# Last layer of a decoder trunk: the residual stored to the output early, and the experts' rows added to it by indirect DMAs, one per expert of a unit and one behind the other

## The reference, cut to what matters

```
def hybrid_layer(x, ...):
    ...
    h = x + mix @ w_o
    return h + hierarchical_moe(rmsnorm(h, norm2_g), w_rg, b_rg, w_re, b_re, w1, w3, w2)

def hierarchical_moe(...):
    # top-1 of 4 groups, then top-2 of its 8 experts: 2 experts a token, 32 in all, no capacity limit
    def expert_block(args):
        xb, e = args
        hid = jax.nn.silu(xb @ w1[e]) * (xb @ w3[e])      # 1024 -> 256
        return hid @ w2[e]                                  # 256 -> 1024
    ...
    y = jnp.zeros((T, d), xn.dtype).at[buf_tok].add(ybuf * buf_gate[:, None])
```

## Time and profile before

| | |
|---|---|
| median of 3 runs (lowest, highest) | 2005.02 us (2003.66, 2007.26) |
| profiled execution, first to last instruction (span) | 2003.5 us |
| PE busy | 1841.7 us (92%) |
| DVE, ACT, POOL busy | 712.4, 555.0, 327.6 us |
| DMA, mean over the span | 163 GB/s, 325.73 MB |
| last layer: h part, unit part, adding | about 1534 to 1685, 1685 to 1968, 1968 to 2003.5 us |

### The profile page before, as it was taken

How to read it: one execution, slowest core, us unless ns; L and a number is a source line. 1 busy time by engine, 2 the same in 40 slices (tenths; PEclk the granted TensorE clock), 3 DMA queues, 4 the chain that set the end, 5 groups by cost and what they waited for, 6 DMA issues and landing times. The chain is left out here.

```text
span 2003.5 us, 29201 instructions
## 1 busy us (share of the span) xinstructions
PE 1841.7 (92%) x11200; PEld 1013.5 (51%) x11200; DVE 712.4 (36%) x2085; ACT 555.0 (28%) x1313; POOL 327.6 (16%) x372
## 2 busy tenths in 40 slices
PE   7999998999899889998699999899998997999992
PEld 4555555776645443333255555567675554433330
DVE  0111105667634522222212221266764443222224
ACT  2121216665612211110121111266563222111010
POOL 0332321011100011111013332310210000111110
PEclk9999998999999989999899999999999997999996
DMA  7000000002061289999752110100203315999997
GB/s 262 11 22 11 0 21 32 1 1 96 2 260 64 105 318 415 423 417 416 277 176 84 43 53 0 53 2 1 85 12 129 147 64 215 356 422 422 415 364 305
DMA packets 93208, 325.73 MB, mean 163 GB/s; under 512 B 19856, under 2 KB 33808, under 8 KB 76688
## 3 DMA queue, kind: packets, MB, share of 16 engines
q1 hardware_dynamic: 70416, 272.97, 34.9%
q0 software_dynamic: 12096, 33.57, 4.2%
q10 hardware_dynamic: 10560, 17.33, 2.5%
HBM read 295.52 MB, written 38.80 MB: 167 GB/s over the span
## 5 line engine op out<-in xcount | busy, mean ns | idle before, releaser
L437 PE MATMUL banks<-r_win,r_tile 128*128 128x384 f32 (+3 forms) x1536 | 531.4, 505 | 9.4 <-DMA r_win<-in_w_in 7.2
L437 PEld LDWEIGHTS banks<-r_win,r_tile 128*128 128x128 f32 x1536 | 292.7, 192 | 226.8 <-issue 61.6
L1827 PE MATMUL banks<-r_win,r_proj 128*32 128x512 f32 (+2 forms) x1184 | 255.3, 606 | 7.9 <-DVE r_proj L2148 4.3
L1675 PE MATMUL banks<-r_proj,r_tile 128*128 128x512 f32 x512 | 238.2, 607 | 0.2 <-DVE r_proj L2098 0.2
L1107 ACT ACTIVATE r_win<-r_win 128x256 f32<-128x256 f32 (+7 forms) x256 | 177.3, 695 | 28.3 <-DVE r_win L1179 20.7
L1827 PE MATMUL banks<-r_proj 128*32 128x512 f32 (+1 forms) x736 | 157.1, 596 | 8.7 <-DMA r_win<-in_w 3.8
L990 PE MATMUL banks<-r_win 64*128 64x512 f32 (+3 forms) x704 | 136.1, 506 | 19.6 <-DVE r_win L1151 10.3
L1675 PEld LDWEIGHTS banks<-r_proj,r_tile 128*128 128x128 f32 x512 | 93.1, 193 | 94.2 <-issue 93.7
L1001 PE MATMUL banks<-fixed,r_win 128*128 128x128 f32 x984 | 132.4, 280 | 6.6 <-ACT r_win L1115 6.5
L1001 PEld LDWEIGHTS banks<-fixed,r_win 128*128 128x128 f32 x984 | 106.2, 141 | 49.5 <-issue 42.8
L507 ACT ACTIVATE r_proj<-banks,rx 128x384 f32<-128x384 f32 (+1 forms) x80 | 48.1, 601 | 297.2 <-PE banks L437 297.2
(11 more groups left out here) (229 smaller groups left out, 2114.9 us busy)
## 6 DMA issues: line engine op xcount, KB each, us to landing
r_win<-in_w SPq DMA_DIRECT2D x99, 1024.0 KB, 18.5
r_proj<-in_w SPq DMA_DIRECT2D x60, 1024.0 KB, 21.6
r_tile<-in_w SPq DMA_DIRECT2D x33, 1024.0 KB, 19.0
r_win<-in_w_in SPq DMA_DIRECT2D x6, 1536.0 KB, 18.3
r_proj<-in_w_o SPq DMA_DIRECT2D x2, 4096.0 KB, 13.4
residual<-r_tile ACTq DMA_DIRECT2D x16, 512.0 KB, 2.9
out<-r_tile SPq DMA_DIRECT2D x16, 512.0 KB, 8.2
r_win<-expert_rows SPq DMA_DIRECT2D x16, 512.0 KB, 9.7
```

Of the source, the lines that this page charges most:

```text
L437: mm = pe.matmul(bk[b][:, 0:CHUNKS[c]], uT[j][:, k, :], w_ch[c][:, k, :], start=(k == 0), stop=(k == KT - 1))
L1675: mm = pe.matmul(bk[2 * (t % 2) + c][:, :], mix[t][:, k, :], s.w_o[:, k, 512 * c:512 * c + 512], start=(k == 0), stop=(k == KT - 1))
L1827: mm = pe.matmul(bk[2 + j][at, 0:2 * F].rearrange("p (c n) -> p c n", c=2), xT[j][:, k, at], w13[c][:, :, k, :], start=(k == 0), stop=(k = ...
```

## The change

1. In the last layer ACT stores each tile of `h` a second time, to `out`, right behind the store to `residual` (in `scale`). SP (before its loads of the experts 5 and 6) and POOL (before its first gather) wait until all 8 of these have landed.
2. The scatter of a unit to `expert_rows` becomes `add_rows`: for each expert of the unit (each "piece") one indirect DMA from the same `y_t` buffer to `out`, which adds instead of overwriting (`compute_op=ALU.add`). A new table `piece_rows` has the slots of the other piece past the end, so that they are left out; it costs one more DVE operation and one more wait behind `rows_out`, in both layers, and a constant table of 42 columns in `fixed`. Each of these DMAs is issued only when the one before it has landed: the second piece of a unit waits for the first, the first for the last piece of the unit before. There are 2 units of one piece and 19 of two, so 40 such DMAs.
3. `first_half` and `second_half` wait, before they overwrite a `y_t` buffer, for both pieces of unit n-2.
4. The reload of `h`, the read-back, the adds on DVE and the stores to `out` at the end are gone. The pass ends when all pieces have landed.
5. `cum`, a small table of the attention, moves into the weight buffer to make room, and counters are added for the passes of this layer.

```
@@ scale
                 act.dma_start(rows(s.h_dram, t), h_t[t]).then_inc(g.hs.sem, 16)
+                if last_layer:
+                    act.dma_start(rows(s.out_f, t), h_t[t]).then_inc(g.os.sem, 16)
@@ block.sync
                 sp.wait_ge(g.hs.sem, g.hs.at(layer, 16 * NT))
+                if last_layer:
+                    sp.wait_ge(g.os.sem, 16 * NT)
...
-                        else:
-                            for t in tiles_at_sets(s):
-                                sp.dma_start(h_t[t], rows(s.h_dram, t)).then_inc(g.hb.sem, 16)
...
-            if last_layer:
-                for t in range(NT):
-                    for k in range(2):
-                        sp.dma_start(yg[t][k], rows(s.y_dram, k * NT + t)).then_inc(g.yg[t].sem, 16)
-                for t in range(NT):
-                    sp.wait_ge(g.ad.sem, 2 * (t + 1))
-                    sp.dma_start(rows(s.out_f, t), h_t[t]).then_inc(g.st.sem, 16)
-                sp.wait_ge(g.st.sem, 16 * NT)
@@ block.gpsimd
+            if last_layer:
+                wait_alone(pool, s, g.os.sem, 16 * NT)
+            def add_rows(n):
+                j, col = n % 2, units[n].col
+                for i in range(len(units[n].pieces)):
+                    if i > 0:
+                        wait_alone(pool, s, g.ac[j].sem, g.ac[j].at(here, added(units, n) - 16))
+                    elif n > 0:
+                        wait_alone(pool, s, g.ac[1 - j].sem, g.ac[1 - j].at(here, added(units, n - 1)))
+                    nc.gpsimd.indirect_dma_start(
+                        out=s.out_f, out_offset=bass.IndirectOffsetOnAxis(
+                            ap=piece_rows[:, U * i + col:U * i + col + 1], axis=0),
+                        in_=y_t[j], in_offset=None, bounds_check=NT * P - 1, oob_is_err=False,
+                        compute_op=ALU.add).then_inc(g.ac[j].sem, 16)
...
-                        scatter(n - 4)
+                        if last_layer:
+                            add_rows(n - 4)
+                        else:
+                            scatter(n - 4)
@@ first_half (second_half the same with dve)
                     if n >= 2:
-                        act.wait_ge(g.ys[j].sem, g.ys[j].at(done, 16 * (n // 2)))
+                        wait_rows_out(act, n - 2)
@@ new
+    def wait_rows_out(eng, n):
+
+        j = n % 2
+        if last_layer:
+            eng.wait_ge(g.ac[j].sem, g.ac[j].at(count_here(eng), added(units, n)))
+        else:
+            eng.wait_ge(g.ys[j].sem, g.ys[j].at(count(eng), 16 * (n // 2 + 1)))
+
+def added(units, n):
+
+    return 16 * sum(len(u.pieces) for u in units[n % 2:n + 1:2])
@@ rows_out
                 v.scalar_tensor_tensor(out=slot_rows[:, 0:U], in0=row_less, scalar=SKIP, in1=bk[0][:, 0:U],
-                                       op0=ALU.add, op1=ALU.add).then_inc(g.ix.sem, 1)
+                                       op0=ALU.add, op1=ALU.add).then_inc(g.sr.sem, 1)
+                wait_alone(dve, s, g.sr.sem, n)
+                ins = v.tensor_tensor(piece_rows.rearrange("p (i u) -> p i u", i=2),
+                                      bcast(slot_rows[:, 0:U].unsqueeze(1), [P, 2, U]),
+                                      s.other_piece.rearrange("p (i u) -> p i u", i=2), ALU.add)
+                ins.then_inc(g.ix.sem, 1)
@@ after the last unit, DVE
-            if last_layer:
-                for t in range(NT):
-                    dve.wait_ge(g.yg[t].sem, 32)
-                    for k in range(2):
-                        v.tensor_tensor(h_t[t], h_t[t], yg[t][k], ALU.add).then_inc(g.ad.sem, 1)
```

More of the change, by code:

```diff
@@ L90, in trunk @@
         banks = [bank_pairs[b // 2][:, 512 * (b % 2):512 * (b % 2) + 512] for b in range(8)]
-        fixed = sb("fixed", [P, 5 * P + 2 * NT * (NROPE // 2) + 1 + 2 * NT + 2])
+        units_n = len(plan_units(E)[0])
+        fixed = sb("fixed", [P, 5 * P + 2 * NT * (NROPE // 2) + 1 + 2 * NT + 2 + 2 * units_n])
         ident, ones, upto, before = (fixed[:, n * P:(n + 1) * P] for n in range(4))
         iota = fixed[:, 4 * P:5 * P]
-        after = itertools.accumulate((5 * P, NT * NROPE, 1, 2 * NT, 1, 1))
-        cos_sin, pick, targets, key_col, expert_col = (fixed[:, a:b] for a, b in itertools.pairwise(after))
+        after = itertools.accumulate((5 * P, NT * NROPE, 1, 2 * NT, 1, 1, 2 * units_n))
+        cos_sin, pick, targets, key_col, expert_col, s_other = (fixed[:, a:b] for a, b in itertools.pairwise(after))
         cos_sin = cos_sin.rearrange("p (a t c) -> p a t c", a=2, t=NT)
@@ L117, in trunk @@
         fox = sb("fox", [P, 3, NT, HEADS])
-        cum = sb("cum", [P, NT, HEADS])
+        cum = r_win[:, 19104:19136].rearrange("p (t h) -> p t h", h=HEADS)
         nrounds = sb("nrounds", [1, 1], I32)
@@ L216, in trunk @@
         s.rounds_done = rounds_done
-        s.reloads = nc.sync.alloc_register("reloads")
         s.attend_sems = attend_sems
         s.route_sems = route_sems
+        s.rounds_here = {e.engine: e.alloc_register("rounds_here") for e in (nc.sync, nc.scalar, nc.vector, nc.gpsimd, nc.tensor)}
         s.rounds = {e.engine: e.alloc_register("rounds") for e in (nc.sync, nc.scalar, nc.vector, nc.gpsimd, nc.tensor)}
@@ L1328, in __init__ @@
         self.col, self.ranks, self.slots = col, ranks, slots
+        self.pieces = [(blocks[0][0], blocks[-1][1]) for blocks in slots]
 def plan_units(experts_n):
@@ L1429, in route_signals @@
     g.ys = [sig(f"expert_rows_stored{j}", 16 * even[j]) for j in range(2)]
+    g.ac = [sig(f"expert_rows_added{j}", added(units, U - 2 + (U + j) % 2)) for j in range(2)]
+    g.os = sig("output_seeded", 16 * NT)
     g.nv = sig("next_pass_places_ready", 2 * NT)
@@ L1527, in count, with count_here, wait_all_rows_out @@
         return eng.snap(s.rounds_done[eng.engine])
+    def count_here(eng):
+        return eng.snap(s.rounds_here[eng.engine])
+    def wait_rows_out(eng, n):
[4 more added lines that the diff above has]
+            eng.wait_ge(g.ys[j].sem, g.ys[j].at(count(eng), 16 * (n // 2 + 1)))
+    def wait_all_rows_out(eng):
+        for j in range(2):
+            if last_layer:
+                wait_alone(eng, s, g.ac[j].sem, g.ac[j].at(count_here(eng), g.ac[j].per_pass))
+            else:
+                wait_alone(eng, s, g.ys[j].sem, g.ys[j].at(count(eng), g.ys[j].per_pass))
     def next_round(eng):
         eng.reg_add(s.rounds_done[eng.engine], s.rounds_done[eng.engine], 1)
+        eng.reg_add(s.rounds_here[eng.engine], s.rounds_here[eng.engine], 1)
         eng.wait_ge(g.nr.sem, g.nr.at(layer, 4))
@@ L1652, in _ @@
             with passes(pool):
-                done = count(pool)
+                done, here = count(pool), count_here(pool)
                 wait_alone(pool, s, g.ix.sem, g.ix.at(done, 1) + layer)
@@ L1931, in _ @@
                 if not last_layer:
-                    for j in range(2):
-                        wait_alone(act, s, g.ys[j].sem, g.ys[j].at(done, g.ys[j].per_pass))
+                    wait_all_rows_out(act)
                 next_round(act)
@@ L2156, in second_half @@
                     if n >= 2:
-                        dve.wait_ge(g.ys[j].sem, g.ys[j].at(done, 16 * (n // 2)))
+                        wait_rows_out(dve, n - 2)
                     v.tensor_scalar(y_t[j][:, 512:1024], bk[7][:, :], slot_gates[:, col:col + 1], None,
@@ L2205, in _ @@
                 second_half(U - 1)
-                for j in range(2):
-                    wait_alone(dve, s, g.ys[j].sem, g.ys[j].at(done, g.ys[j].per_pass))
+                wait_all_rows_out(dve)
                 dve.wait_ge(g.p1.sem, g.p1.at(done, 1))
@@ L2255, in tables @@
     copies = np.where(p // experts_n == 1, -FIRST_KEY, np.tile(keys, P // experts_n))
+    units = sorted(plan_units(experts_n)[0], key=lambda u: u.col)
+    other = np.full((2, len(units), P), SKIP)
+    for u in units:
+        for i, (a, b) in enumerate(u.pieces):
+            other[i, u.col, a:b] = 0
+    other = other.reshape(-1, P)
     fixed = [np.eye(P), np.ones((P, P)), p[:, None] <= p[None, :], p[:, None] < p[None, :],
              np.tile(p, (P, 1)), cs.reshape(P, -1), p[:, None] % HD == 0, targets,
-             copies[:, None], p[:, None] % experts_n]
+             copies[:, None], p[:, None] % experts_n, other.T]
     return {
```

22 lines of the change are left out of this document (7 added, 15 removed).

## The result

The changed kernel takes **2083.52 us** in the median (2076.39 to 2091.87, 4 runs) against 2004.34 (4 runs) before it: ratio 1.040, 95% interval 1.037 to 1.043. Slower by 1.7% was forecast; it is slower by 4.0%. The time lies inside the range (1995 to 2090) and more than twice as far from the kernel before as the forecast had it, next to the rival *dear adds* (2081). The profiled execution has a span of 2090.0 us. It took 2091.87 us, 8.4 more than the median and the longest of its four, so sums made from this trace end some 8 us late.

The account below looks back on a forecast made before the run. In the unit part PE and DMA race and DMA wins; the read-back follows. Removing the tail gives 35.7 us back, the chain ends the units 69 us later: 2038.5 us, 1.7% slower, range 1995 to 2090 for 8 in 10.

Parts of the forecast that it names:

- dear adds: Rival, 20%: in the chain, old rows queue among the weights like new ones; links 14.5 us loaded, 5.1 idle; median 2081.
- The addition itself is in no row: Chain of adds: adding to rows standing in `out` costs 0.6 us a link, sized by 8.39 MB more to read.
- the chain with the addition free: Lower bound for the unit part: addition free, no old rows; 21.5 loaded and 16.5 idle links, median 2013.5 us.
- the forecast's own sum: From the third unit's scatter: 217.4 us DMA work, 22.0 loaded links at 9.9, 16.0 idle at 4.7; 292.6 us.
- What goes: End of the kernel: everything after the last scatter's landing goes, 35.7 us, of which 1.7 us remains as the pass's end.
- Early stores: In the h part: eight more 512 KB stores on ACT's queue cost nothing; without cover 3 us, once.
- The gap: Chain of adds: from one landing to POOL's next issue, 0.9 us a link.
- Small piece as long as a large one beside the weights: Chain of adds: a 32-row piece still carries 96 empty slots, so it gets the large piece's landing time, 8.4 us loaded.
- DMA work of the old rows: Unit part: reading the old rows of 19 units, 7.3 MB, adds 17.7 us to 199.7 us of DMA work.
- Clock: PE in the unit part: lower granted clock costs nothing; under 0.8 there was named a sign of being wrong.
- Gathers and DMA share: Signs in the unit part: gathers 15 us apart instead of 12.3, DMA's share about 0.75, last weight at 1970 or later.
- Rival hidden: Rival, 17%: adds keep up with PE, the last weight sets the end; medians 1979 to 1997, faster by 0.4 to 1.3%.

Follow-up runs that it names:

- experiments 4 and 5: 4: changed kernel with each DMA naming only its own partitions, 2042.60 us; 5: the same with plain scatters instead of adds, 2000.40 us.
- Experiment 1: Changed kernel with its 40 chained DMAs as plain scatters that overwrite instead of adding: 2025.91 us, ratio 1.010 to the kernel before.
- experiment 8: Kernel before plus only the early stores of `h` to `out` and the waits for them: 2006.22 us, ratio 1.000.
- experiment 7: Changed kernel with the plain, unchained scatters of before to `expert_rows`, and no read-back or adds at the end: 1973.05 us, ratio 0.984 to the kernel before.
- experiment 6: Changed kernel with all row numbers of both pieces past the end, so its 40 chained adding DMAs move no rows: 2008.79 us, ratio 1.001 to the kernel before.

## Why the prediction was wrong

The mechanism was right: the chain sets the pace, throttles PE and the weights, and ends last. The step that failed is a size, in the forecast's words "The addition itself is in no row" and "I take 0.6 us a link". It is 2.2 us loaded (10.3 against 8.1, or 1.9 without a chain), and 2.8 and 1.9 idle. I had sized it by the bytes of the old rows alone, 0.9 us for a large piece and a third of it for a small one. That leaves out the longer issue on POOL (0.5 to 0.6 us) and the empty slots, which are dearer in an adding DMA: without them it is 1.8 and 1.0 idle (experiments 4 and 5).

In medians the miss is 45.0 us (2083.5 against 2038.5). The forecast had 2013.5 for the chain with the addition free, and 25.0 more for the addition. Experiment 1 has 2025.9 for the former, 12.4 more than forecast, and so 57.6 for the addition, 32.6 more than forecast. Of the 12.4 one cause is seen in its trace and not in my sum: a pair of idle links (9.4 us in the forecast, 7.6 there) is shorter than PE's 12.26 us a unit, so PE sets the pace at the end. The rest of the 12.4 stays open. In the changed kernel an idle pair takes 12.5 us, and PE is not on the chain.

With the measured terms the forecast's own sum comes out near the trace: DMA work 199.7 + 21.0 = 220.7 us; loaded link 10.3 + 0.85 = 11.15, so 19.8 of them; 18.2 idle at 5.4 + 0.85 = 6.25 make 113.8; together 334.5, or 333.7 without the gap behind the last. The trace has 335.7 from 1750.98 to the last landing at 2086.65. That it agrees so well is in part luck: the same sum misses by 15 us in experiment 1, and the trace has not 19.8 links at 11.15 and then 18.2 at 6.25, but 26 at 10.0 while weights still land and 12 at 6.4 behind them. Against the forecast's end of 2037.3 in the profiled span, 2090.0 is 52.7 later: 44.0 from the links (335.7 against 291.7 up to the last landing), 7.1 from the start (1750.98 against 1743.85; 4.4 of it is there at the first gather, which varies from trace to trace, see experiment 8), 1.6 at the very end.

Point by point:
- *What goes*: 34.0 forecast, 33.5 measured (experiment 7). Right.
- *Early stores*: nothing. Right (experiment 8). The DVE operation with its wait: L2111 to L2114's end is 0.48 us where L2086 alone had 0.18; the 0.3 is as forecast.
- *The gap*: 0.9 forecast, 0.8 to 0.9 between landing and issue. Right (2082.05 - 2075.20 - 6.0).
- *Small piece as long as a large one beside the weights*: true of the first units (10.4 against 10.7, 9.1 against 9.9), not of the whole: over the ten units of 96 and 32 rows from 1773 on it is 7.7 against 10.5 in the mean. So the sign that I gave for the contrary did show, in part beside the weights and clearly without them (4.6 against 6.0). It isn't all a matter of rows: in experiment 6, where both are empty, the second piece of a unit lands in 7.0 us in the mean and the first in 8.3 (six units from 1766 on). Why the second is sooner there was not tested.
- *DMA work of the old rows*: 17.7 forecast, 21.0 measured (21 to 24 with the spread of single traces). Low.
- *Clock*: it was under 0.8 in windows of the unit part (0.74 from 1953 to 1972), which I had named as a sign of being wrong. The term, no cost, is right all the same: PE is not on the chain of waits.
- *Gathers and DMA share*: gathers are 22 us apart at first and 16 to 22 later, not 15, and DMA's share is 0.84 from 1838 to 2001, not 0.75. The last weight lands at 2010.7, "1970 or later".
- *Rival dear adds* (20%): its time, 2081, is the measured one, but by terms that cancel: it had 5.2 us more for an addition beside the weights (2.2 measured) and 1.0 without them (2.8 and 1.9). So its mechanism, old rows queueing like new ones, is not what was seen: in experiment 6 no row is added and the DMA still takes 7.9 us of the 10.3.
- *Rival hidden* (17%): by its own decision point, "a pair under 12.3 us", it falls; the pair was 22.3 beside the weights. The estimate from the Trainium skill's page "DMA: Bandwidth & Descriptors", section "Anatomy of one DMA — SWDGE (gpsimd) path" (2.9 and 2.3 us), is under the adds' 6.0 and 4.6 even with DMA idle; the plain scatters' 3.2 and 2.7 are near it.

The range held the time because it reached into a rival whose mechanism was not the one seen; the point in it stood too near the low bound, since for the one operation without a row I took a value close to that bound.

## What to carry to other kernels

Before indirect DMAs are put one behind the other, multiply their number by the landing time *beside the traffic that will be there* (8.4 us here, not 3.2) and set it against the time of the work that shall hide it. Set the price of a link with DMA idle against that same work too: where it is shorter, the work sets the pace. Give each such DMA only the partitions it moves. An operation that no row shows, as the adding DMA here, is worth one timed run by itself before a whole end is rebuilt on it.

## What the runs showed of the hardware

- An empty slot of an indirect DMA (a row number past the end) is not free beside other traffic: 128 of them in an adding DMA took 7.9 us, against 8.4 for a plain scatter of up to 128 rows, though 5120 of them took only some 4.5 us of the DMA engines' own time. Dropping them took the fifth unit's large link from 10.8 to 9.8 us and its small one from 9.9 to 7.3.
- An adding DMA costs 1.0 us more than a plain one for 32 rows and 1.8 for 96, with DMA idle and no empty slots; with 128 slots named it is 1.9 and 2.8. POOL's issue is 0.5 to 0.6 of it (1.57 against 0.99 us for 128 slots), and as long when every slot is empty.
- The additions of at most 8.39 MB held the last weight up by 21 to 24 us and kept the DMA engines busy for 24 us more than plain scatters of the same bytes, which with the gathers made 41.9. At 412 GB/s 8.39 MB take 20.4 us: for the DMA engines an added row is about two rows or a little more.
